# Last pair of a windowed attention: gate products pulled ahead, two merge steps put between two heads' values, VectorE's large operands placed behind GpSimd's selects

## The reference, cut to what matters

```python
q = rms_norm(q.reshape(b, s, N_Q_HEADS, HEAD_DIM), q_norm_g)
k = rms_norm(k.reshape(b, s, N_KV_HEADS, HEAD_DIM), k_norm_g)
o = sliding_window_attention(q, k, v, sinks) * jax.nn.silu(z_a)
y_b = jnp.einsum('bsc,cd->bsd', o, w_attn_out)
gates = jax.nn.sigmoid(gate_logits + gate_b)
g_a, g_b = jnp.split(gates, N_BRANCHES, axis=-1)
merged = g_a * y_a + g_b * y_b
return x + jnp.einsum('bsd,de->bse', merged, w_out)
```

## Time and profile before

| what | before |
|---|---|
| median of 3 runs | 2462.91 us (2462.41 to 2463.95) |
| the profiled execution's own time | 2462.61 us |
| span of its trace, first to last instruction | 2460.4 us |
| outside the span | 2.2 us |
| PE busy | 2422.4 us (98%) |
| DVE, POOL, ACT busy | 1543.8, 1366.0, 1088.5 us |
| granted TensorE clock | 1.000 of full speed |

### The profile page before, as it was taken

How to read it: one execution, slowest core, us unless ns; L and a number is a source line. 1 busy time by engine, 2 the same in 40 slices (tenths; PEclk the granted TensorE clock), 3 DMA queues, 4 the chain that set the end, 5 groups by cost and what they waited for, 6 DMA issues and landing times. The chain is left out here.

```text
span 2460.4 us, 35738 instructions
## 1 busy us (share of the span) xinstructions
PE 2422.4 (98%) x11516; PEld 1995.9 (81%) x11516; DVE 1543.8 (63%) x2247; ACT 1088.5 (44%) x2010; POOL 1366.0 (56%) x1220
## 2 busy tenths in 40 slices
PE   8999999999999999999999999999999999999999
PEld 5888888888788878888888888777878888878877
DVE  6555552344677786435666666656868777777885
ACT  4332333401666661116777777731432333344441
POOL 3798887534455564343222222254279888666683
PEclk9999999999999999999999999999999999999999
DMA  3222223579210014332111111431133333487652
GB/s 113 90 75 66 72 68 109 181 264 331 89 31 30 26 35 169 131 119 70 61 60 60 60 60 57 155 119 56 44 121 121 112 120 115 147 273 220 188 181 82
DMA packets 128803, 275.64 MB, mean 112 GB/s; under 512 B 14128, under 2 KB 14256, under 8 KB 128704
## 3 DMA queue, kind: packets, MB, share of 16 engines
q1 hardware_dynamic: 84800, 157.85, 20.6%
q10 hardware_dynamic: 43904, 116.58, 13.3%
HBM read 206.41 MB, written 67.96 MB: 112 GB/s over the span
## 5 line engine op out<-in xcount | busy, mean ns | idle before, releaser
L643 POOL TENSOR_SCALAR whi<-raw 128x512 fp32r<-128x512 f32 x194 | 141.4, 729 | 373.3 <-PE bank L853 202.8
L645 POOL TENSOR_TENSOR wlo<-raw,whi 128x512 fp32r<-128x512 f32 x194 | 273.6, 1411 | 16.2
L853 PE MATMUL bank<-a_hi,whi 128*128 128x512 f32 x464 | 182.6, 394 | 1.5 <-issue 1.5
L853 PE MATMUL bank<-b_lo,whi 128*128 128x512 f32 x464 | 181.4, 391 | 0.0
L658 POOL TENSOR_TENSOR wlo<-a,whi 128x512 fp32r<-128x512 f32 x114 | 161.2, 1414 | 24.5 <-ACT whi L1759 24.2
L916 PE MATMUL bank<-b_hi,whi 128*128 128x512 f32 x384 | 156.8, 408 | 0.2 <-ACT f_raw L1579 0.2
L916 PE MATMUL bank<-b_hi,wlo 128*128 128x512 f32 x384 | 150.6, 392 | 0.0
L916 PE MATMUL bank<-b_lo,whi 128*128 128x512 f32 x384 | 150.1, 391 | 0.0
L761 POOL COPY fc<-fc 128x128 f32<-128x128 f32 x96 | 29.0, 302 | 192.0 <-DVE mx L2572 191.9
L853 PE MATMUL bank<-b_hi,whi 128*128 128x512 f32 x336 | 131.6, 392 | 0.5 <-DVE b_lo L2374 0.4
L853 PE MATMUL bank<-a_hi,wlo 128*128 128x512 f32 x336 | 130.8, 389 | 0.0
(11 more groups left out here) (710 smaller groups left out, 7722.7 us busy)
## 6 DMA issues: line engine op xcount, KB each, us to landing
raw<-in_w SPq DMA_DIRECT2D x206, 256.0 KB, 2.6
a<-in_pairs SPq DMA_DIRECT2D x152, 256.0 KB, 2.7
fc<-c_scr ACTq DMA_DIRECT2D x32, 512.0 KB, 3.6
wd_scr<-wd SPq DMA_DIRECT2D x55, 256.0 KB, 5.0
wd<-in_down SPq DMA_DIRECT2D x44, 256.0 KB, 4.6
xs_scr<-made ACTq DMA_DIRECT2D x40, 256.0 KB, 2.6
h_scr<-up_y ACTq DMA_DIRECT2D x13, 512.0 KB, 2.6
raw<-wd_scr SPq DMA_DIRECT2D x26, 256.0 KB, 3.1
```

Of the source, the lines that this page charges most:

```text
L643: nc.gpsimd.tensor_scalar(hi, src, 1.0, 1.0, ALU.mult, ALU.mult).then_inc(w_hi, 1)
L645: nc.gpsimd.tensor_tensor(lo, src, hi.bitcast(F32), ALU.subtract).then_inc(w_lo, 1)
L853: last = nc.tensor.matmul(psum_ap, ws[w][:, k, :], a[:, kt, hs(h)], start=(first and i == 0 and j == 0), stop=(final and i == n - 1 and j ...
```

## The change

TensorE: in the last pair, step k = 0 of tile 0 is put ahead of flip_p(3), in both halves, and the rest of the first two steps behind values(2), now with tile 1's second half; after the last values, three ranges of k (2 and 3, 4 and 5, 6 and 7) go over both tiles and halves, where two stood (2 and 3, then 4 to 7). ScalarE: the copies window_hi are ahead by one to four places, and those of pairs 4 and 5 stand inside the last pair, with a wait for its scores. VectorE: window_lo(0) stands between gate(0) and normalise(2), window_lo(1) between maxima(3) and normalise(3); gate(1) and window_lo(2) stand behind a wait for GpSimd's selects of step 2, window_lo(3) and window_lo(4) behind one for those of step 3. GpSimd's and SyncE's streams are the same.

```diff
@@ TensorE, window_pair, last pair
                     fill(1, 1, range(4, 6))
+                    for h in range(2):
+                        merge_part(0, h, range(1))
                     flip_p(3)
                     fill(1, 1, range(6, KT))
                     values(2)
-                    for c, h in ((0, 0), (0, 1), (1, 0)):
-                        merge_part(c, h, range(2))
+                    for h in range(2):
+                        merge_part(0, h, range(1, 2))
+                    for h in range(2):
+                        merge_part(1, h, range(2))
                     values(3)
@@ TensorE, after the pairs
-            merge_part(1, 1, range(2))
-            for ks in (range(2, KH), range(KH, KT)):
+            for ks in (range(2, 4), range(4, 6), range(6, KT)):
                 for c in range(2):
                     for h in range(2):
                         merge_part(c, h, ks)
@@ ScalarE, window_hi
-                act.wait_ge(sw.pv, NW * (NPAIR - 1 if j < 4 else NPAIR))
+                act.wait_ge(sw.pv, NW * (NPAIR - 1 if j < 6 else NPAIR))
+                if j in (4, 5):
+                    act.wait_ge(sw.scored, NW * NPAIR)
@@ ScalarE, window_pair, last pair
+                    window_hi(0)
                     gate_a(0)
+                    window_hi(1)
                     expo(2)
                     fold(0)
                     high(1)
-                    window_hi(0)
+                    window_hi(2)
+                    window_hi(3)
                     expo(3)
                     fold(1)
                     high(2)
-                    window_hi(1)
+                    window_hi(4)
                     gate_a(1)
                     fold(2)
                     high(3)
-                    window_hi(2)
-                    window_hi(3)
+                    window_hi(5)
                     fold(3)
@@ VectorE, window_pair, last pair
                     gate(0)
+                    window_lo(0)
                     normalise(2)
                     add(0)
                     low(1)
                     maxima(3)
-                    window_lo(0)
+                    window_lo(1)
                     normalise(3)
                     add(1)
                     low(2)
-                    window_lo(1)
+                    dve.wait_ge(sw.parted, st * 4 + 12)
                     gate(1)
+                    window_lo(2)
                     add(2)
                     low(3)
-                    window_lo(2)
+                    dve.wait_ge(sw.parted, st * 4 + 16)
                     window_lo(3)
+                    window_lo(4)
                     for hh in range(2):
                         gated(hh, 0)
                     gated(0, 1)
```

More of the change, by code:

```diff
@@ L1982, in _ @@
                 window_pair(NPAIR // 2 - 1, pp)
-            for j in range(4, NPAIR):
+            for j in range(6, NPAIR):
                 window_hi(j)
@@ L2851, in _ @@
                 window_pair(NPAIR // 2 - 1, pp)
-            for j in range(4, NPAIR):
+            for j in range(5, NPAIR):
                 window_lo(j)
```

## The result

The changed kernel takes 2466.93 us (median of 22 runs, 2464.05 to 2469.19), the kernel before on the same chips 2463.36 (22 runs, 2460.89 to 2466.57). The ratio is 1.0015, 95% interval 1.0009 to 1.0020: slower by 3.6 us, less than 0.2%. The forecast was 2465.6, from a sum of +2.7 us, with a range of 2462.0 to 2467.8. The profiled execution took 2466.66 us, with a span of 2464.0 where it was 2460.4.

The account below looks back on a forecast made before the run. PE, busy 98% of the span, was taken to bound the kernel, so only its idle time counts: 3.17 us taken away against 0.2, 1.45, 0.35, 1.5 and 2.4 added gives +2.7, so 2465.6 us, range 2462.0 to 2467.8.

Parts of the forecast that it names:

- (a) to (c): PE idle time taken away: 0.77 us ahead of flip_p(3), 1.19 in values(2), about 1.0 of 1.21 in values(3).
- (e): Merge step k = 3: PE waits for b_hi 3, held by GpSimd's whi; +0.35 us, 0 with no meeting.
- (g): Ahead of tile(U_AOUT + 2): fewer steps cover GpSimd's weight split; +2.4 us idle, bounds 2.05 and 3.0.
- (f): Merge step k = 5: PE waits for b_hi 5, behind other VectorE work; +1.5 us, between 0.3 and 1.9.
- (d): b_hi 0 between gate(0) and normalise(2) meets GpSimd's wlo; flip_p(2) comes 1.45 us later, 1.0 if the product precedes the select.
- the sign that was named for (d): At flip_p(2): about 2.1 us idle, and the sp product that releases it stretched to over 1 us.
- The faster one: Rival: VectorE's and GpSimd's operations miss each other in their new places; -1.1 us, 2461.8; chance 0.13.
- The slower one: Rival: VectorE bounds the merge, three gate products taking 3.83 us beside the split; +4.4 us, 2467.3; chance 0.14.
- What follows is paced by PE, so the shift stays to the end: Behind 936 us: PE idles only in short waits on its neighbours, so the +2.7 us reaches the end unchanged.
- the fall as a rival: Granted clock falls to 1.2 GHz at the idle time ahead of tile(U_AOUT + 2); about 5 us more, 2470; chance 0.02.

Follow-up runs that it names:

- tail_only: The kernel before with only the merge's last ranges of k changed to 2-3, 4-5, 6-7: 2465.78 us, ratio 1.0014.
- after_lo5: The changed kernel with the subtraction of pair 5 ahead of the last gate products, not behind them: 2465.84 us, ratio 1.0011.
- lo0_only: The kernel before with only the copy and subtraction of pair 0 pulled ahead to their new places: 2462.93 us, ratio 1.0003.
- after_early_half: The changed kernel, with GpSimd splitting the first half of the third tile's weights once tile 0 has used steps 0 to 3: 2465.17 us, ratio 1.0014.
- after_again: The changed kernel run once more, unaltered: 2467.08 us, ratio 1.0021 against the kernel before.
- after_lo0_back: The changed kernel with the subtraction of pair 0 back between maxima(3) and normalise(3): 2466.94 us, ratio 1.0022.
- best_up_filled: best_half with eight added matmuls that enter no output ahead of the up projection: 2460.14 us, ratio 0.9989.
- after_both_filled: The changed kernel with added matmuls that enter no output, nine ahead of the bank and eight ahead of the up projection: 2464.87 us, ratio 1.0010.
- before_up_filled: The kernel before with eight added matmuls that enter no output ahead of the up projection: 2461.84 us, ratio 0.9997.
- best_order: after_lo0_back with subtraction 2 behind low(3), 5 ahead of the gate products, and six steps of tile 1 behind tile 0: 2461.49 us, ratio 0.9996.
- best_half: best_order's VectorE order, after_early_half's early split, and k = 2 to 5 step by step over both tiles: 2459.79 us, ratio 0.9992.

## Why the prediction was right, and where it was off

**The waits, (a) to (c), (e) to (g).** Each came at the place and from the releaser that was named, within 0.2 us of its size. tail_only shows (g) by itself, after_lo5 (f): it takes that wait away and nothing else grows. (g) is above its lower bound for the reason given: the first sums of the merge now meet the split's middle, and its second whi takes 1.07 us where it took 0.62 before (the wlo behind it was held before too, 1.60 us, and takes 1.58 now). In after_lo5, where that whi takes 0.63, the wait is 1.88.

**(d), the right mechanism at the wrong end of its bounds.** I took 1.45 because "GpSimd's next select asked at 901.29; so it is first". After, the select asked just then (900.98, in an execution that is 0.31 ahead), and the product at 900.98 too; it kept its 0.69, the select took 1.18, and the term is 0.94, where the working named 1.0 if the product gets in ahead. So the sign that was named for (d), a product of over 1 us, did not show. lo0_only shows 0.95 for this part alone. The product was early because the working put 0.43 us between the end of wlo and its request; row_sum, though, ends with wlo (900.73 and 900.71), and the product follows 0.25 behind. The Trainium skill ("SBUF — State Buffer", section "Who interferes with whom") says that whoever issues first has the shared port pair for its whole instruction and the other is blocked. The rows agree: 1.21 for b_hi 0, 2.22 for wlo behind it, 1.12 for a row_sum of 128x4 behind that.

**The rivals.** The faster one failed where the text said it would: flip_p(2) waits 1.58 us, not 0.7. The slower one failed too: the three gate products took 2.11 us, not 3.83, since the split's wlo had ended (at 918.68, and they begin at 919.68); after_early_half shows that the mechanism is real once a split is put there.

**"What follows is paced by PE, so the shift stays to the end"**: this sentence is the step that missed 1.3 us. Its ground, idle time "in short waits" after 936 us, was misread: the kernel before already has a wait of 2.00 us at 1808.05. The shift grew from 2.4 to 4.0 us at this gap, which the change doesn't touch, when the granted clock fell to half behind it; 0.7 us of that was made up again by the last matmul, and some 0.65 us came behind it. That the forecast's +2.7 lies as near to 3.6 as it does is in part luck: (d) was taken 0.5 us too large.

The prediction had the fall as a rival, at the new gap, with a chance of 2 in 100 and a price of about 5 us. At the new gap the clock fell in two of the five profiles that have it unfilled (1.88 to 2.62 us: tail_only and after_again, not the changed kernel's first profile, after_lo5 or after_lo0_back), and the one fall that is taken apart above cost 1.6 us; a slow stretch of some 10 us shows in no run. The argument against was the first 5 us, in which PE did nothing at a clock of 1.00. Those 5 us were no evidence for the rest, and the sentence that no row shows a fall was wrong: the kernel before has one in its last 5.4 us, where PE stands idle behind the last matmul, and best_up_filled's last 4.8 us, PE as idle, stood at 0.68.

```profile
2455.00:2460.40 5.40, 0.56 (x3) 0.14 (x1) 1.45 (x2) 0.69 (x1) 0.00 (x0) 0.83 0.26 99
```

The table of the experiments speaks for the clock: in the six kernels without a fall in the profile, the median moved by the stretch, give or take a microsecond (-1.05 to +0.7 besides it); in the six with one, and in the changed kernel itself, it lies 0.9 to 3.4 us above what the stretch gives, of which up to 0.65 us can be the time behind the last matmul. That is a relation over single profiles and medians of other executions, with intervals of 2.2 us to either side, so the size is not shown for each kernel. The kernel before shows the same within itself: on the three chips its executions with a mean clock of 1.000 have medians of 2461.36, 2461.41 and 2462.24 us, those with 0.999 2463.72, 2463.02 and 2464.34, 1.6 to 2.4 us more (after_both_filled's 11 executions show no such difference). That the fall hangs on the gap is what the counts point to, no more: with the up projection's gap open, seven of eleven profiles lost the clock there (that of the changed kernel among them, that of the kernel before not); with it filled, none of three did. The Trainium skill ("TensorE: Matmul & The Clock Gate", Part 1) has an idle array fall back to half its clock; after_again's 0.74 behind 2.31 us is such a fall, the changed kernel's first profile, 1.00 behind 2.32 us, shows none.

**What stays open.** Why the same gap brings the fall in one execution and not in another, and so why the kernel before was spared in its profile. With a gap of 2.00 us there it may lose the clock in some of its own runs; its 33 runs beside the last four kernels spread over 4.4 us, those of before_up_filled, 11 runs, over 1.7, but three times as many runs spread further by chance too. Open is also what makes the 0.65 us behind the last matmul.

## What to carry to other kernels

Work pulled ahead to fill waits moves the end of its own tile too: count what stands behind the last use of a buffer before and after, since that was the cover of the next load or split. Here 3.1 us were gained in three small waits and 5.3 lost in four others, most of which best_order and best_half undid by leaving more behind tile 0 or splitting its weights earlier, putting the operand that is wanted first ahead of the gate products, and keeping long SBUF to SBUF work out of the way from a gate to a normalisation. And when a kernel loses more than the stretch that was changed, look at the granted clock behind each gap of 2 us or so, also those far from the change, and at what the run spends behind its last matmul.

## What the runs showed of the hardware that was not expected

- The granted clock fell to half behind gaps of 2.0 to 2.7 us in a TensorE that is busy for 98% of the span, in some executions only, while others of 2.00 to 2.52 us passed at full clock; one fall cost about 1.6 us, in the changed kernel's profile.
- Very small VectorE operations are held as long as large ones: row_sum of 128x4 took 1.12 us behind a wlo, 0.19 without.
- After a gap at full clock the first matmul of 128x512 is followed 0.33 us later, not 0.23, so each wait costs 0.1 us more than the idle time shown.
- The time outside the span goes by the kernel: 2.1 us in the median of the three with the early split, 2.2 in the kernel before and the three made from it, 2.5 to 2.6 in the changed kernel and the others made from that. In no kernel do its runs differ by more than 0.2 us in it.
